# HGRN attention by doubling and an fp32 input projection without splits, in a two-layer hybrid trunk on one core

## The reference

```
x = x + 1/2 * SwiGLU_1(RMSNorm(x))            # 1024 -> 2816 -> 1024
h = RMSNorm(x); p = h @ W_in                  # combined input projection
x = x + concat(A, B, C) @ W_out
x = x + 1/2 * SwiGLU_2(RMSNorm(x))
```

```
f = lb + (1 - lb) * sigmoid(f_logit);  key = 1 - f
S_t = diag(f_t) S_{t-1} + key_t i_t^T;  o_t = S_t^T q_t
```

## Time and profile before

| | |
|---|---|
| median of 3 runs | 1140.01 us (1139.86 to 1148.8) |
| profiled execution | 1146.21 us, span 1144.4 us |
| mean granted TensorE clock | 0.972 |
| PE / DVE / ACT / POOL busy | 1087.5 / 691.3 / 548.7 / 335.5 us |
| stage of the input projection and head groups, layer 0 | 211.93 to 354.92 us |
| the same, layer 1 | 769.26 to 918.29 us |
| output projection, layer 0 | 354.92 to 382.36 us |

### The profile page before, as it was taken

How to read it: one execution, slowest core, us unless ns; L and a number is a source line. 1 busy time by engine, 2 the same in 40 slices (tenths; PEclk the granted TensorE clock), 3 DMA queues, 4 the chain that set the end, 5 groups by cost and what they waited for, 6 DMA issues and landing times.

```text
span 1144.4 us, 22655 instructions
## 1 busy us (share of the span) xinstructions
PE 1087.5 (95%) x9020; PEld 1057.7 (92%) x9020; DVE 691.3 (60%) x764; ACT 548.7 (48%) x635; POOL 335.5 (29%) x375
## 2 busy tenths in 40 slices
PE   4999999969989999999999999998799899999997
PEld 4999999968888999999999999998788789999997
DVE  4767655678751665555668656575966335545557
ACT  5664434635633644344475544454563336344345
POOL 3199920335620100000015997012544101000001
PEclk9999999989979999999999999999896999999999
DMA  8354554322231454455445454443132134544542
GB/s 319 138 218 186 184 186 181 112 100 99 98 111 56 170 217 184 184 183 183 180 169 221 157 210 184 172 158 111 75 111 74 74 120 164 220 186 160 199 180 95
DMA packets 26131, 181.07 MB, mean 158 GB/s; under 512 B 3024, under 2 KB 4048, under 8 KB 4560
## 3 DMA queue, kind: packets, MB, share of 16 engines
q1 hardware_dynamic: 25488, 176.18, 41.9%
q10 hardware_dynamic: 288, 2.99, 0.7%
q0 software_dynamic: 288, 1.05, 0.2%
HBM read 179.15 MB, written 1.05 MB: 157 GB/s over the span
## 4 chain that ended last, share of the span: by engine, by line
issue 50%; PE 29%; POOL 12%; DVE 7%; ACT 2%; DMA 1%; POOLq 0%; SPq 0%; DVEq 0%; ACTq 0%
PE ps L822 7%; PE ps L823 7%; PE ps L824 7%; PE ps L1182 5%; POOL in_lo L537 2%; POOL sumsq L416 1%; DMA raw<-stream 1%; DVE qk L1475 1%; DVE lo L1213 1%; POOL sin L450 1%; ACT hi L575 1%; POOL w_lag L521 0%; DVE bc L1523 0%; POOL cos L452 0%; DVE dec L1462 0%
## 5 line engine op out<-in xcount | busy, mean ns | idle before, releaser
L1213 DVE TENSOR_TENSOR lo<-raw,hi 128x2048 fp32r<-128x2048 f32 x134 | 312.9, 2341 | 286.6 <-ACT hi L575 286.6
L822 PE MATMUL ps<-xg_hi,hi 128*128 128x256 f32 x1408 | 401.5, 285 | 20.2 <-DVE lo L1213 18.1
L823 PE MATMUL ps<-xg_lo,hi 128*128 128x256 f32 x1408 | 399.8, 284 | 0.0
L824 PE MATMUL ps<-xg_hi,lo 128*128 128x256 f32 x1408 | 399.8, 284 | 0.0
L575 ACT ACTIVATE hi<-raw 128x2048 fp32r<-128x2048 f32 x134 | 255.1, 1908 | 244.5 <-PE ps L824 213.7
L822 PEld LDWEIGHTS ps<-xg_hi,hi 128*128 128x128 f32 x1408 | 271.6, 193 | 21.1 <-DVE lo L1213 18.5
L823 PEld LDWEIGHTS ps<-xg_lo,hi 128*128 128x128 f32 x1408 | 271.7, 193 | 0.3
L824 PEld LDWEIGHTS ps<-xg_hi,lo 128*128 128x128 f32 x1408 | 271.5, 193 | 0.0
L822 PE MATMUL ps<-act_hi,hi 128*128 128x256 f32 x704 | 199.6, 284 | 0.9 <-DVE act_lo L1250 0.9
L823 PE MATMUL ps<-act_lo,hi 128*128 128x256 f32 x704 | 199.4, 283 | 0.0
L824 PE MATMUL ps<-act_hi,lo 128*128 128x256 f32 x704 | 199.4, 283 | 0.0
(11 more groups left out here) (307 smaller groups left out, 1478.8 us busy)
## 6 DMA issues: line engine op xcount, KB each, us to landing
raw<-stream SPq DMA_DIRECT2D x164, 1024.0 KB, 4.8
par<-params ACTq DMA_DIRECT2D x2, 1458.0 KB, 7.6
rows<-stream SPq DMA_DIRECT2D x2, 1024.0 KB, 6.7
x<-xT SPq DMA_DIRECT2D x2, 512.0 KB, 4.9
out<-x SPq DMA_DIRECT2D x8, 128.0 KB, 1.8
con<-consts POOLq DMA_DIRECT2D x1, 513.5 KB, 8.7
trig_tmp<-masks POOLq DMA_DIRECT2D x1, 512.0 KB, 10.3
g<-gain SPq DMA_DIRECT2D x1, 4.0 KB, 1.6
```

What stands on the lines that cost most here:

```text
L822: pe.matmul(acc, w_hi, a_hi, start=start, stop=False, skip_group_check=True)
L823: pe.matmul(acc, w_hi, a_lo, start=False, stop=False, skip_group_check=True)
L824: return pe.matmul(acc, w_lo, a_hi, start=False, stop=stop, skip_group_check=True)
L1213: v.tensor_tensor(lo[slot][:, :], raw[slot][:, :], hi[slot][:, :].bitcast(F32), ALU.subtract).then_inc(lo_written, 1)
```

## The change

**Projection.** w_in and h are no longer split. `project` and `project_tokens` multiply the fp32 tile in `raw` and the fp32 `h` (written by ScalarE alone) with one matmul in place of three; the forget logits likewise. TensorE waits for the unit's load itself, and `in_used` counts whole units: the SP queue refills a slot when TensorE has used the unit. All `split_in` on ScalarE, VectorE and GpSimd, the split of w_forget, and GpSimd's clearing of `attn` are gone.

**HGRN.** The levels go from block size 1 up to 64. f itself is used, without logs or exponentials. `span[j]` holds products of f over aligned blocks of 2, 4, ... 64 tokens, each from the one before. Level 0 is the diagonal (key, bq), written to `attn` through a product with the identity. `qd` starts as bq times f, and `key` as 1 - f; before level n + 1, `extend(n)` multiplies in place the q of every second block and the key of every first block of size `LEVELS[n - 1]` by the product of the neighbouring block. An extend waits for its level's matmuls, which read what it overwrites, and raises `kq_ready` for the next level. Level 8 is the product of the halves. The matmul shapes of the levels stay, their places in TensorE's and VectorE's lists move.

```diff
-LEVELS = [64, 32, 16, 8, 4, 2, 1]
-NLEV = len(LEVELS) + 1
-NSTEP = NLEV + 1
+LEVELS = [1, 2, 4, 8, 16, 32, 64]
+NLEV = len(LEVELS)
+NSTEP = NLEV + 2
...
-                        wait_in_split(w - RING)
+                        sp.wait_ge(in_used, l * IN_UNITS + w - RING + 1)
                     load(l * UNITS + FFN_UNITS + w, w % RING)
                 for w in range(OUT_UNITS):
                     if w < RING:
-                        wait_in_split(IN_UNITS - RING + w)
+                        sp.wait_ge(in_used, l * IN_UNITS + IN_UNITS - RING + w + 1)
...
-                split_in((len(POOL_UNITS) - 1) * QUARTERS)
...
-                        e.activation(h_hi[:, m, :], x[:, m, :], ACT.Copy, scale=gain[:, m:m + 1]
-                                     ).then_inc(h_hi_ready, 1)
+                        e.activation(h[:, m, :], x[:, m, :], ACT.Copy, scale=gain[:, m:m + 1]
+                                     ).then_inc(h_ready, 1)
...
-                split_in(8)
                 e.wait_ge(proj_dve, l * 9 + 3)
                 e.activation(key[:, :, :], bf[:, :, :], ACT.Sigmoid).then_inc(bf_sig, 1)
-                split_in(4)
-                e.wait_ge(bf_f, l + 1)
-                e.activation(bf[:, :, :], bf[:, :, :], ACT.Ln).then_inc(bf_log, 1)
-
-                def decays(n):
...
-                def quarter_ready(n, part):
-                    pe.wait_ge(in_lo_pool if n in POOL_UNITS else in_lo_dve, in_split_count(l, n, part))
+                def unit_loaded(n):
+                    pe.wait_ge(raw_loaded[n % RING], (l * VISITS + ITERS + n // RING + 1) * 16)
...
-                            pe.wait_ge(h_lo_ready, l * KT + k + 1)
+                            pe.wait_ge(h_ready, l * KT + k + 1)
                         for m in range(2):
-                            last = three(b[:, m * T:(m + 1) * T], in_hi[part][:, w + m * P:w + m * P + P],
-                                         in_lo[part][:, w + m * P:w + m * P + P], h_hi[:, k, :], h_lo[:, k, :],
-                                         k == 0 and m == 0, k == KT - 1)
-                        if k % 2 == 1:
-                            last.then_inc(in_used, 1)
+                            last = pe.matmul(b[:, m * T:(m + 1) * T],
+                                             raw[n % RING][:, k * 256 + m * P:k * 256 + m * P + P], h[:, k, :],
+                                             start=k == 0 and m == 0, stop=k == KT - 1, skip_group_check=True)
+                    last.then_inc(in_used, 1)
 
...
-                            tok = slice(t * P, (t + 1) * P)
-                            last = three(b[:, t * 256:(t + 1) * 256], h_hi[:, k, tok], h_lo[:, k, tok],
-                                         in_hi[part][:, w:w + 256], in_lo[part][:, w:w + 256],
-                                         k == 0 and t == 0, k == KT - 1)
-                        if k % 2 == 1:
-                            last.then_inc(in_used, 1)
+                            last = pe.matmul(b[:, t * 256:(t + 1) * 256], h[:, k, t * P:(t + 1) * P],
+                                             raw[n % RING][:, k * 256:(k + 1) * 256],
+                                             start=k == 0 and t == 0, stop=k == KT - 1, skip_group_check=True)
+                    last.then_inc(in_used, 1)
 
...
-                    if n < NLEV - 1 or n == NSTEP - 1:
-                        pe.wait_ge(qk_ready, l * (NSTEP - 1) + (n if n < NLEV - 1 else n - 1) + 1)
+                    pe.wait_ge(kq_ready, l * (NSTEP - 1) + max(n, 1))
...
+                        if n == NSTEP - 1:
+                            last = pe.matmul(b[:, hd * P:(hd + 1) * P], key[:, hd, 0:P], qd[:, hd, P:T],
                                              start=True, stop=True, skip_group_check=True)
...
+                            if n == 0:
+                                last = pe.matmul(b[:, i * P:(i + 1) * P], key[:, hd, tok], bq[:, hd, tok],
+                                                 start=True, stop=True, skip_group_check=True)
+                            else:
+                                c = qd[:, hd, tok].rearrange("p (n s k) -> p n s k", s=2, k=LEVELS[n - 1])
+                                last = pe.matmul(b[:, i * P // 2:(i + 1) * P // 2], key[:, hd, tok], c[:, :, 1, :],
+                                                 start=True, stop=True, skip_group_check=True)
...
-                project(6, {1: lambda: level(0), 4: s5_glu})
+                project(6, {1: lambda: level(0), 3: lambda: level(1), 5: s5_glu})
                 pe.wait_ge(sg_ready, l + 1)
-                pe.wait_ge(forget_ready, l + 1)
                 for k in range(KT):
-                    last = three(bank(7)[0:4, 0:T], forget_hi[:, k * 4:k * 4 + 4], forget_lo[:, k * 4:k * 4 + 4],
-                                 h_hi[:, k, :], h_lo[:, k, :], k == 0, k == KT - 1)
+                    last = pe.matmul(bank(7)[0:4, 0:T], prm("w_forget", k * 4, 4), h[:, k, :], start=k == 0,
+                                     stop=k == KT - 1)
                 last.then_inc(af_done, 1)
-                level(1)
                 pe.wait_ge(af_abs, l + 1)
-                project_tokens(7)
-                level(2)
-                project_tokens(8, {2: lambda: fox_sums(0), 3: lambda: fox_sums(1)})
-                level(3)
-                project_tokens(9, fox_scores(1, 2))
-                level(4)
-                level(5)
-                project(10, fox_scores(0, 2))
-                level(6)
+                project_tokens(7, {2: lambda: level(2), 5: lambda: level(3)})
+                project_tokens(8, {1: lambda: level(4), 3: lambda: fox_sums(0), 4: lambda: fox_sums(1),
+                                   6: lambda: level(5)})
+                project_tokens(9, {1: lambda: level(6), **fox_scores(1, 2)})
+                level(7)
+                project(10, {1: lambda: level(8), **fox_scores(0, 2)})
                 fox_transposes(1)
-                level(7)
-                level(8)
                 hgrn_output()
                 project(11, {2: lambda: fox_transposes(0), 3: hgrn_sums, 6: fox_output})
...
-                    v.wait_ge(h_hi_ready, l * KT + m + 1)
-                    v.scalar_tensor_tensor(h_lo[:, m, :], x[:, m, :], gain[:, m:m + 1], h_hi[:, m, :].bitcast(F32),
-                                           ALU.mult, ALU.subtract).then_inc(h_lo_ready, 1)
...
+                def extend(n):
+
+                    v.wait_ge(lev_done, l * NSTEP + n + 1)
+                    size, f = LEVELS[n - 1], span[n - 1]
+                    if n == NLEV:
+                        v.tensor_tensor(qd[:, :, T - size:], qd[:, :, T - size:],
+                                        f[:, :, 2:3].broadcast_to([P, HEADS, size]), ALU.mult)
+                        v.tensor_tensor(key[:, :, 0:size], key[:, :, 0:size],
+                                        f[:, :, 1:2].broadcast_to([P, HEADS, size]), ALU.mult).then_inc(kq_ready, 1)
                         return
+                    blocks = [P, HEADS * T // (2 * size), size]
+                    pair = f[:, :, :].rearrange("p h (n s) -> p (h n) s", s=2)
+                    q = qd[:, :, :].rearrange("p h (n s k) -> p (h n) s k", s=2, k=size)[:, :, 1, :]
+                    k = key[:, :, :].rearrange("p h (n s k) -> p (h n) s k", s=2, k=size)[:, :, 0, :]
+                    v.tensor_tensor(q, q, pair[:, :, 0:1].broadcast_to(blocks), ALU.mult)
+                    v.tensor_tensor(k, k, pair[:, :, 1:2].broadcast_to(blocks), ALU.mult).then_inc(kq_ready, 1)
 
...
+                        v.tensor_tensor(attn[:, :, :], b.rearrange("p (i t) -> p i t", t=P),
+                                        ident.unsqueeze(1).broadcast_to([P, 2 * HEADS, P]), ALU.mult
+                                        ).then_inc(lev_read, 1)
+                        return
...
-                st.wait()
-                v.tensor_scalar(bf[:, :, :], bf[:, :, :], 2.0 ** -63, None, ALU.max).then_inc(bf_f, 1)
                 take(3, bq[:, 0:2, :])
-                v.wait_ge(bf_log, l + 1)
-                for hd in range(HEADS):
-                    last = v.tensor_tensor_scan(bc[:, hd, :], carry, bf[:, hd, :], 0.0, ALU.mult, ALU.add)
-                st.mark(last)
-                st.wait()
-                st.mark(v.tensor_tensor(bsum[:, :].unsqueeze(2), bc[:, :, CHUNK - 1:CHUNK],
-                                        bc[:, :, 2 * CHUNK - 1:2 * CHUNK], ALU.add))
-                exponents(0)
-                exponents(1)
+                for small, large in zip(span, span[1:]):
+                    pair = small[:, :, :].rearrange("p h (n s) -> p (h n) s", s=2)
+                    st.mark(v.tensor_tensor(large[:, :, :].rearrange("p h n -> p (h n)").unsqueeze(2),
+                                            pair[:, :, 0:1], pair[:, :, 1:2], ALU.mult))
+                    st.wait()
                 take(4, bq[:, 2:4, :])
-                v.wait_ge(bf_f, l + 1)
                 v.wait_ge(proj_dve, l * 9 + 5)
```

(53 more changed lines are left out.)

195 lines of the change are left out of this document (23 added, 172 removed).

## The result

The changed kernel takes 1126.15 us (median of 4 runs, 1125.56 to 1126.74), the kernel before 1144.40 beside it (4 runs, 1139.86 to 1150.36). The ratio is 0.985 with a 95% interval of 0.980 to 0.989: faster by about 1.5%. The difference of the medians is 18.3 us. The profiled execution took 1125.56 us around a span of 1123.8, against 1146.2 and 1144.4.

A forecast was written before the change was run, and what follows sets the result against it. TensorE's own instructions bound the stage, with 29.4 us of waits and 25.0 of half clock on top. Work 133.3, waits 3.3 and clock 3.0 make 139.6 us a layer, 12.8 less for both: 1127 us, range 1113 to 1146.

The forecast's parts named there:

- The products: Projection and forget logits: 200 native fp32 products cost 86.4 us a layer, 14.5 more than the split matmuls.
- All other work: TensorE's remaining work in the projection and head-group stage, by subtraction: 46.9 us a layer, taken as unchanged.
- The 9 us wait: TensorE's wait before unit 4 for its split, 9.0 us a layer: gone, with unit 2 taken by 241.5.
- The other waits: TensorE's waits left in the stage after the change: 3.3 us a layer, 1.9 and 1.4.
- Forget chain: Four VectorE instructions that TensorE awaits, no longer covered by level 1: 1.9 us, at the other end 4.0.
- cross level: Wait before level 8, where extend(7) stands behind the mask and `scores(6)` on VectorE: 0.9 us.
- The clock: TensorE's half-clock loss in the stage: 3.0 us a layer taken, between bounds of nothing and 12.5.
- rival 1: Clean clock in the stage: no dip, 2.3 us of waits, 135.6 us a layer, 20.8 less, 1119 us; chance 0.20.
- The sum: Both stages: 139.6 us a layer, 279.2 against 292.0, 12.8 less; 1127 us after a 6.2 us profile-to-median step.
- Clock as before: Half clock in the stage stays at 9.3 and 15.7 us, 19 more than forecast, 1146 us; chance 0.15.
- Slower by ping-pong: Slow or late extends add 12 us a layer over seven levels, clock falls as before, 1170 us; chance 0.07.
- Waits that only change their name: Unit banks, weights or scan hold TensorE as the splits did; 29 us more, 1169 us; chance 0.05.

The follow-up runs named there:

- native_scores: `split_tuned` with units 9 and 10, in the score stretch, multiplied natively in fp32; 1115.38 us, ratio 0.977.
- mixed: Split products in units 0, 1 and 4 to 8, native fp32 in 2, 3, 9, 10, 11, forget wait late; 1110.81 us, ratio 0.972 against the kernel before.
- native_only: The kernel before with the native fp32 projection alone, old attention in its old order; 1130.30 us, ratio 0.992.
- doubling_only: The changed kernel with the split projection and all its splits put back, new attention kept; 1136.33 us, ratio 0.995.
- held_take: The changed kernel with ten idle VectorE additions a layer ahead of the take of unit 2; 1149.92 us in one run.
- pool_busy: The changed kernel with forty 128x512 subtractions a layer on GpSimd that nobody waits for; 1135.29 us in one run.
- late_wait: The changed kernel with TensorE's forget wait moved from before unit 7 to the sums of unit 8; 1124.65 us, ratio 0.984.
- split_tuned: `doubling_only` with unit 3 split by GpSimd, unit 4 split by ScalarE before the sigmoid, forget wait at unit 8; 1134.46 us, ratio 0.993.

## Why the prediction was right, and where it was not

**The products.** Predicted 86.4 us a layer, from 0.216 a record and 32 records a unit. Measured 0.219 over unit 0 and 88 records in one uninterrupted row; right to 1.5%. That the change adds work, 29 us, was right too, and `native_scores` and `mixed` show it from the other side.

**All other work.** Predicted 46.9 us a layer, measured 136.1 - 86.4 - 2.3 = 47.4. The 2 us that the end of switching between the two kinds of tiles might have saved are not seen.

**The 9 us wait.** Predicted gone, with the scan ended by 240.8 and unit 2 taken by 241.5; measured 240.90, and no wait. Its cause was shown from both sides: `native_only` has no such wait, `doubling_only` still waits 9.0 us, and `held_take` makes it again.

**The other waits.** Forget chain 1.9 predicted, 1.9 measured. Level 6 predicted 0.2, none; cross level 0.9, measured 0.4; transposes 0.3, none in the list. In sum 3.3 predicted, 2.3 measured. Where the rows before left two ends open, the short ones came true (0.34 and 0.69 us), and `pool_busy`, in which GpSimd works again, has the long ones back (0.96, 1.35 and 1.52).

**The clock.** This is the term that was mis-sized: 3.0 us a layer taken, 0.0 measured. The first reason given, that the dip after the 9 us wait has nothing to follow, held. The second, that the reordered levels leave more native tiles in the scores of the second block, was half of it: `native_only`, whose levels are not reordered, loses only 1.5 and 1.7 us, and `doubling_only`, whose levels are, still loses 10.3 and 7.3. The native projection, with the splits and waits that it takes away, counts for more than the order. What came true is the clean clock of rival 1, to which the prediction gave 0.20, with its 2.3 us of waits: 135.6 us a layer where 136.1 were measured, and its 20.8 us less are the span's 20.6. The 3.0 us were not out of reach for these tiles: `late_wait` loses 1.7 and 3.4. The prediction also speaks of two small losses of 1.7 us before; its own rows have three, and its sums of 9.3 and 15.7 count all three.

**The sum.** The forecast of 1127 lies 0.9 from the median, and that closeness is luck: two errors cancel in it. The stages gave 19.8 us instead of 12.8, 7.0 more. But the step from the profiled execution to the median, 6.2 us, was carried over from the kernel before, and does not belong to the one after. Every run has its mean clock beside it, and that explains most of the step:

| kernel | runs, us | clock of the run |
|---|---|---|
| before | 1136.8, 1139.5, 1141.8, 1146.7 | 0.981, 0.978, 0.975, 0.971 |
| `native_only` | 1128.5, 1130.3, 1137.3, 1139.7 | 0.997, 0.995, 0.990, 0.987 |
| after | 1125.6, 1126.3, 1126.7 | 0.999, 0.998, 0.998 |

The profiled execution of before had 0.972, and a run at 0.978 took 6.7 us less, which is the step of 6.2 in its size. A run's time moves with its clock: in `native_only` 11.2 us for 0.010, which is 11.3 us of its span. The four runs of the kernel after have next to no half clock to vary, hence they agree within 1.2 us where those before scatter over 10.5. Its profiled execution stands 0.6 us below its median, not 6.2 above: 6.8 us the other way. Against the kernel before as measured beside it, the gain is 18.3 us and the forecast had 13.

**The other rivals.** Clock as before, 1146: refuted, the stretch is at 1.00 in both layers. Slower by ping-pong, 1170: refuted, extends of 0.69 us in gaps of two or three tiles; even with GpSimd at work it cost 9.7 us (`pool_busy`, one run). Waits that only change their name, 1169: refuted by 2.3 us in place of 14.7. Of the conditions that would have made the forecast wrong, none occurred.

**What stays open.** Which property of the score stretch holds TensorE at half clock for 31 us while it is busy was narrowed, not settled: native units 9 and 10 end it, and split ones in an otherwise native stage show 7 us, about what native tiles alone did in `late_wait` (4 and 7 us). Making those two units native also removes the two short waits right before the stretch; moving only these waits was not tried. `doubling_only`, which has them without the long stretch, speaks against them as the whole cause. The edit also takes the two units' splits from ScalarE and GpSimd; the short losses of `pool_busy` (4.6 and 1.7) speak against GpSimd as the cause, and ScalarE's part was not tried alone.

## What to carry to other kernels

Before pricing an edit on a busy TensorE, take the busy time by stretch with the granted clock beside it: here the half clock (25.0 us) was nearly as large as all waits together (29.4), and a change that adds 29 us of TensorE work gained 20. Work that feeds TensorE through other engines has three prices, its instructions, the waits, and the neighbours that it slows; choose the form unit by unit by what runs beside it, as the mixed version does. A clean clock in four runs is a finding on that one version: moving a single wait brought some half clock back. And when executions of a kernel scatter, read each one's clock, and do not carry the distance from profile to median over to a kernel whose clock behaves otherwise.

## What the runs showed of the hardware that had not been expected

TensorE was held at 1.2 GHz for 31.5 us on end while the profile counts it busy for all of them (`split_tuned`, clock 0.51); with two of its twelve units native, and two short waits gone with that, the same stretch ran at 2.4 GHz in layer 0 (clock 1.00) and had 7.5 us at half clock in layer 1. Removing its last idle time did not raise its clock: `late_wait`, busy for 135.37 us of 135.37, lost 1.7 us to half clock where the kernel with 2.3 us of waits lost none, in one profiled execution of each. Beside GpSimd the scan took 3.27 us for 2.29, a product of SBUF tiles 1.35 to 1.78 for 0.69, and GpSimd's own split 15.71 / 8 = 1.96.
